# Attention on one core: two passes of 80 steps become one of 160, with the V product every second step, the softmax scaling on GpSimd and the first turned group evicted by VectorE

## The reference

```
def attend(q, k, v, scale):
    s = jnp.einsum('bhgqd,bhkd->bhgqk', q, k).astype(jnp.float32) * scale
    p = jax.nn.softmax(s, axis=-1).astype(v.dtype)
    return jnp.einsum('bhgqk,bhkd->bhgqd', p, v)
```

## Time and profile before

| | |
|---|---|
| time, 3 runs | 4382.3 us median (4377.97 to 4382.8) |
| profiled execution | span 4381.5 us from its first to its last instruction; no other time of this execution is given |
| busy in the span | PE 3800.6 us (87%), DVE 1762.5 (40%), ACT 1253.8 (29%), POOL 114.2 (3%) |
| granted TensorE clock, mean | 0.929 |
| attention, kind 0 | scores from 514.9 us, last product done by 813.8 |
| attention, kind 1 | scores from 831.1 us, last product done by 1165.3 |
| in kind 0 (298.9 us) | PE 260.69 busy, DVE 184.33, ACT 207.47, POOL 0 |
| in kind 1 (334.2 us) | PE 297.14 busy, DVE 187.29, ACT 213.36, POOL 0 |

### The profile page before, as it was taken

How to read it: one execution, slowest core, us unless ns; L and a number is a source line. 1 busy time by engine, 2 the same in 40 slices (tenths; PEclk the granted TensorE clock), 3 DMA queues, 4 the chain that set the end, 5 groups by cost and what they waited for, 6 DMA issues and landing times. The chain is left out here.

```text
span 4381.5 us, 45125 instructions
## 1 busy us (share of the span) xinstructions
PE 3800.6 (87%) x17768; PEld 2756.6 (63%) x17768; DVE 1762.5 (40%) x2388; ACT 1253.8 (29%) x2132; POOL 114.2 (3%) x80
## 2 busy tenths in 40 slices
PE   6687788788886999999996997749899878999997
PEld 2464366566674888888875685513344456888885
DVE  0321566555407333333345333953133234333334
ACT  2322467566524111111123132211100132221122
POOL 0000000000001000000000001300000010000001
PEclk7898899899997999999998998858999898999998
DMA  7532410110012111111122210021310121111112
GB/s 282 199 132 79 96 37 13 49 29 20 25 44 96 39 38 38 38 38 38 38 77 87 75 37 7 1 83 39 123 45 24 48 87 53 48 48 48 48 48 91
DMA packets 98138, 272.32 MB, mean 62 GB/s; under 512 B 18157, under 2 KB 33005, under 8 KB 93972
## 3 DMA queue, kind: packets, MB, share of 16 engines
q1 hardware_dynamic: 98004, 270.51, 18.5%
HBM read 220.41 MB, written 50.07 MB: 62 GB/s over the span
## 5 line engine op out<-in xcount | busy, mean ns | idle before, releaser
L514 PE MATMUL psum<-h_high,w_high 128*128 128x512 f32 (+1 forms) x1280 | 473.5, 370 | 51.5 <-DVE w_low L593 51.5
L514 PE MATMUL psum<-h_low,w_high 128*128 128x512 f32 (+1 forms) x1280 | 473.1, 370 | 0.0
L514 PE MATMUL psum<-h_high,w_low 128*128 128x512 f32 (+1 forms) x1280 | 472.5, 369 | 0.0
L527 PE MATMUL psum<-hid_low,w_high 128*128 128x512 f32 (+1 forms) x1280 | 471.6, 368 | 0.0
L527 PE MATMUL psum<-hid_high,w_high 128*128 128x512 f32 (+1 forms) x1280 | 471.3, 368 | 0.0
L527 PE MATMUL psum<-hid_high,w_low 128*128 128x512 f32 (+1 forms) x1280 | 470.8, 368 | 0.0
L458 PE MATMUL psum<-h_high,w_high 128*128 128x512 f32 (+1 forms) x944 | 368.1, 390 | 50.8 <-DMA swap_halves<-in_swap_a_dram 26.3
L590 DVE TENSOR_TENSOR out<-out,psum 128x512 f32<-128x512 f32 x320 | 202.9, 634 | 463.1 <-PE psum L527 463.1
L458 PE MATMUL psum<-h_high,w_low 128*128 128x512 f32 (+1 forms) x944 | 349.4, 370 | 0.0
L458 PE MATMUL psum<-h_low,w_high 128*128 128x512 f32 (+1 forms) x944 | 349.3, 370 | 0.0
L540 ACT ACTIVATE w_high<-w_raw 128x1024 fp32r<-128x1024 f32 x126 | 132.7, 1053 | 663.2 <-PE psum L527 662.8
(11 more groups left out here) (309 smaller groups left out, 5562.0 us busy)
## 6 DMA issues: line engine op xcount, KB each, us to landing
w_raw<-in_ff_w_dram SPq DMA_DIRECT2D x128, 512.0 KB
ada_ring<-in_ada_w_dram SPq DMA_DIRECT2D x24, 2048.0 KB, 10.8
scratch_x<-x SPq DMA_DIRECT2D x6, 2048.0 KB, 7.2
x<-scratch_x SPq DMA_DIRECT2D x6, 2048.0 KB
x<-in_x_dram SPq DMA_DIRECT2D x4, 2048.0 KB
w_raw<-in_w_out_dram SPq DMA_DIRECT2D x16, 512.0 KB
scratch_spectra<-spectrum_out SPq DMA_DIRECT2D x32, 256.0 KB, 2.0
filter_ring<-scratch_spectra SPq DMA_DIRECT2D x16, 512.0 KB, 3.7
```

The source lines that it names most:

```text
L514: mm = pe.matmul(g.ps[:, u % BANKS, 0:n], x[:, k, :], y[:, k, a:a + n], start=(k == 0 and i == 0), stop=(k == KT - 1 and i == 2))
L527: mm = pe.matmul(g.ps[:, BANKS + u % BANKS, 0:n], x[:, k * 2 + half, :], y[:, k, a:a + n], start=(k == 0 and i == 0), stop=(k == HT - 1 an ...
```

## The change

- One run over 8 pairs (4 of kind 0, then 4 of kind 1), `N` = 160 steps, in one set of buffers and semaphores. The first items of kind 1 are made ready during the last pair of kind 0: items are split at 25 steps instead of 21, besides the first pair's.
- A block is now 128 queries of both heads, 2 steps. `mix` is due in every even iteration and has 20 products of 128 columns instead of 256. The number of scores and transposes is the same.
- The turns lag 3 steps behind the scores (`LAG`) instead of 2. PE's order in an iteration becomes: scores of the first two banks, the first group of 4 transposes of x-3, the product if due, scores of the third bank, the other two groups.
- DVE copies the first turned group out of PSUM (L1195 in the new file), at the start of its iteration. ACT keeps the other two groups (L1253), and the product's result (L1248).
- GpSimd scales the probabilities (L1214) in place of DVE. DVE keeps maximum (L1200), reciprocal (L1206) and `split_item` (L1187).

```diff
-    ALL = [(pair, i) for pair in range(PAIRS) for i in range(S)]
+    ALL = [(pair, i) for pair in range(KINDS * PAIRS) for i in range(S)]
...
+    def block_due(x):
+        return (x - LAG - 2) // 2 if x % 2 == 0 and LAG + 2 <= x + 1 and 0 <= (x - LAG - 2) // 2 < N // 2 else None
+
+    use, act_turns = {}, {}
+    for x in range(N + LAG + 3):
+        if 0 <= x - LAG < N:
+            use["turn", x - LAG, 0] = len(use)
+        if block_due(x) is not None:
+            use["mix", block_due(x)] = len(use)
+        if 0 <= x - LAG < N:
+            for j in range(1, len(turns(x - LAG))):
+                use["turn", x - LAG, j] = len(use)
+                act_turns[x - LAG, j] = len(act_turns)
...
-                    for x in range(N + 3):
-                        if x < N:
-                            scores_of(x)
-                        if x > 2 and (x - 2) % PER_BLOCK == 0:
-                            mix((x - 3) // PER_BLOCK)
-                        if 2 <= x < N + 2:
-                            turn(x - 2)
...
+                def bank_free(r):
+                    if r < 2:
+                        return
+                    key = user[r - 2]
+                    if key[0] == "mix":
+                        pe.wait_ge(mixed_out, key[1] + 1)
+                    elif key[2] == 0:
+                        pe.wait_ge(first_out, key[1] + 1)
+                    else:
+                        pe.wait_ge(turned_out, act_turns[key[1], key[2]] + 1)
...
+                def mix(y):
+                    pair, b, _ = step(2 * y)
+                    lo, hi = keys_of(b)
+                    r = use["mix", y]
+                    bank_free(r)
+                    pe.wait_ge(first_out, 2 * y + 2)
+                    if act_turns_until(2 * y + 1):
+                        pe.wait_ge(turned_out, act_turns_until(2 * y + 1))
+                    pe.wait_ge(v_in[pair % 2], v_total(pair))
+                    for kt in range(lo, hi):
+                        for h in range(HEADS):
+                            mm = pe.matmul(g.ps[64 * h:64 * h + 64, 6 + r % 2, 0:P], v[:, pair % 2, kt, h, :], pt[:, y % 2, h, kt, :],
+                                           start=(kt == lo), stop=(kt == hi - 1))
+                    mm.then_inc(filled, 1)
+
+                for x in range(N + LAG + 3):
+                    if x < N:
+                        scores_of(x, 0, 2)
+                    if 0 <= x - LAG < N:
+                        turn(x - LAG, 0)
+                    if block_due(x) is not None:
+                        mix(block_due(x))
+                    if x < N:
+                        scores_of(x, 2, 3)
+                    if 0 <= x - LAG < N:
+                        for j in range(1, len(turns(x - LAG))):
+                            turn(x - LAG, j)
+
...
-                    for x in range(N + 1):
-                        if x < N:
-                            dve.wait_ge(scores, x + 1)
-                            if x >= 4:
-                                dve.wait_ge(exped, x - 3)
-                            flat = g.ps[:, 3 * (x % 2):3 * (x % 2) + 3, :].rearrange("p b n -> p (b n)")[:, 0:width(x)]
-                            dve.tensor_reduce(neg_max[:, x % 4:x % 4 + 1], flat, AX.X, ALU.max, negate=True).then_inc(maxed, 1)
-                        if x >= 1:
-                            y = x - 1
-                            dve.wait_ge(exped, y + 1)
-                            if y >= 4:
-                                dve.wait_ge(probs, y - 3)
-                            dve.reciprocal(inv[:, y % 4:y % 4 + 1], total[:, y % 4:y % 4 + 1]).then_inc(inverse, 1)
-                            dve.wait_ge(inverse, y + 1)
-                            dve.tensor_scalar(p[:, y % 3, 0:width(y)], p[:, y % 3, 0:width(y)], inv[:, y % 4:y % 4 + 1], None, ALU.mult).then_inc(probs, 1)
-                        if x < N and split_at(x):
-                            split_item(*split_at(x))
...
+                for x in range(N + LAG):
+                    if 0 <= x - LAG:
+                        dst, src = turned_to(x - LAG, 0)
+                        dve.wait_ge(filled, use["turn", x - LAG, 0] + 1)
+                        dve.tensor_copy(dst, src).then_inc(first_out, 1)
+                    if x < N:
+                        dve.wait_ge(scores, x + 1)
+                        if x >= 4:
+                            dve.wait_ge(exped, x - 3)
+                        dve.tensor_reduce(neg_max[:, x % 4:x % 4 + 1], scores_flat(x), AX.X, ALU.max, negate=True).then_inc(maxed, 1)
+                    if 1 <= x <= N:
+                        y = x - 1
+                        dve.wait_ge(exped, y + 1)
+                        if y >= 4:
+                            dve.wait_ge(probs, y - 3)
+                        dve.reciprocal(inv[:, y % 4:y % 4 + 1], total[:, y % 4:y % 4 + 1]).then_inc(inverse, 1)
+                    if x < N and split_at(x):
+                        split_item(*split_at(x))
+
+            @block.gpsimd
+            def _(pool):
+                for y in range(N):
+                    pool.wait_ge(inverse, y + 1)
+                    pool.tensor_scalar(p[:, y % 3, 0:width(y)], p[:, y % 3, 0:width(y)], inv[:, y % 4:y % 4 + 1], None, ALU.mult).then_inc(probs, 1)
...
+                for x in range(N + LAG + 3):
+                    if 1 <= x <= N:
+                        y = x - 1
+                        act.wait_ge(maxed, y + 1)
+                        if y >= 3:
+
+                            act.wait_ge(filled, last_turn(y - 3) + 1)
+                        if y >= 4:
+                            act.wait_ge(inverse, y - 3)
+                        act.activation(p[:, y % 3, 0:width(y)], scores_flat(y), ACT.Exp, bias=neg_max[:, y % 4:y % 4 + 1],
+                                       accum_out=total[:, y % 4:y % 4 + 1]).then_inc(exped, 1)
+                        if split_at(y):
+                            round_item(*split_at(y))
+                    if block_due(x) is not None:
+                        y = block_due(x)
+                        pair, b, _ = step(2 * y)
                         r = use["mix", y]
                         act.wait_ge(filled, r + 1)
-                        act.activation(out[:, kind * PAIRS + pair, b * QB:(b + 1) * QB], g.ps[:, 6 + r % 2, 0:QB], ACT.Copy).then_inc(emptied, 1)
-
-                    for n in range(I):
```

More of the change, by code:

```diff
@@ L1000, in keys_of, with kind_of, step @@
+    COPIES = (2, 1)
+    ROWS = (slice(0, P), slice(0, B_DK))
+    jobs = [(pair, n) for pair in range(KINDS * PAIRS) for n in range(len(ITEMS[pair // PAIRS]))]
+    job_of = {job: m for m, job in enumerate(jobs)}
+    def kind_of(pair):
+        return pair // PAIRS
+    def step(x):
+        pair, i = ALL[x]
+        return pair, i // HEADS, i % HEADS
     def keys_of(b):
-        return (0, KTILES) if b < LAT // QB else (LAT // P, KTILES)
-    def block_of(x):
-        return steps[ALL[x][1]][0]
+        return (0, KTILES) if b < LAT // P else (LAT // P, KTILES)
@@ new lines, in v_total @@
+    def v_total(pair):
+        return 16 * sum(COPIES[kind_of(i)] for i in range(pair % 2, pair + 1, 2))
+    def block_due(x):
[10 more added lines that the diff above has]
+                act_turns[x - LAG, j] = len(act_turns)
@@ L1089, in scores_of @@
                         if x >= 2:
                             pe.wait_ge(exped, x - 1)
-                        kh = 0 if kind == 0 else h
-                        passes = [(q_hi, k_hi), (q_hi, k_lo)] + ([(q_lo, k_hi)] if kind else [])
-                        for j, (a, n) in enumerate(parts):
-                            for m, (left, right) in enumerate(passes):
-                                mm = pe.matmul(g.ps[:, 3 * (x % 2) + j, 0:n], left[rows, s, h, qs], right[rows, s, kh, a:a + n],
-                                               start=(m == 0), stop=(m == len(passes) - 1))
-                            if j == len(parts) - 1:
-                                mm.then_inc(scores, 1)
@@ new lines, in scores_of @@
+                    passes = [(q_hi, k_hi), (q_hi, k_lo)] + ([(q_lo, k_hi)] if kind else [])
+                    for j, (a, n) in list(enumerate(parts))[first:last]:
+                        for m, (left, right) in enumerate(passes):
+                            mm = pe.matmul(g.ps[:, 3 * (x % 2) + j, 0:n], left[at, s, h, qs], right[at, s, kh, a:a + n],
+                                           start=(m == 0), stop=(m == len(passes) - 1))
+                        if j == len(parts) - 1:
+                            mm.then_inc(scores, 1)
@@ new lines, in turned_to, with scores_flat, _, split_item @@
+            def turned_to(x, j):
+                pair, b, h = step(x)
+                lo, hi = turns(x)[j]
+                y, r = x // 2, use["turn", x, j]
+                return pt[:, y % 2, h, lo:hi, :], g.ps[:, 6 + r % 2, 0:(hi - lo) * P].rearrange("p (k n) -> p k n", n=P)
+            def scores_flat(x):
```

(25 more changed lines are left out.)

232 lines of the change are left out of this document (91 added, 141 removed).

## The result

The changed kernel takes 4435.65 us (median of 4 runs, 4433.97 to 4437.33) against 4382.55 for the kernel before on the same chip: a ratio of 1.0127, 95% interval 1.0115 to 1.0139, so 53 us slower. The forecast was 4373, the range ended at 4412. The profiled execution has a span of 4433.7 us. The loss lies in attention: from the first score to the end of the last product it takes about 702 us (516.9 to 1219.1) instead of 650.4, where 641 was forecast.

A forecast was written before the change was run, and what follows sets the result against it. No engine was full for long; PE waited for evictions and, at splits, for DVE. Pairs -24.4, one run -22.3 and splits +37.5 gave -9.2 us against the 4381.5 span, so 4373 us, range 4336 to 4412.

The forecast's parts named there:

- the price of the scaling on GpSimd: Scaling of 1280 columns on GpSimd: taken as 2.41 us, between bounds of 0.887 and 4.08.
- the loop through GpSimd: Kind 0, two steps: maximum, reciprocal, scaling, first group, product, scores; 5.1 + 2.41 = 7.5 us, the longest loop.
- rival 2: GpSimd scaling sets attention's pace; each 0.1 us beyond 2.41 costs 3.2 us in kind 0; 4408 or 4456; chance 0.15.
- Steady state: Attention away from splits: two steps take 7.5 us in kind 0 and 8.4 in kind 1; pairs save 24.4 us.
- The splits: 25 item splits: DVE waits for ACT's rounding, delaying the copy; +57.8 us, +15 for clock, less 35.3 before: +37.5.
- Rival 1: Stalls at splits are milder, 1.7 us for each of 25 items: 4342 us, half way 4358; chance 0.25.
- Rival 3: Each of 25 split stalls drops the clock, +32 us, hand-overs +8: 4412 us; chance 0.16 with the dear product.
- The split that waits for GpSimd: `split_item` waits until the scaling ends: no cost at 2.41 us, 2.5 us for each 0.1 us more on GpSimd.
- One run of 160 steps: Merging both kinds removes the 17.3 us stretch between them and one fill and drain of 5: -22.3 us.
- The signs of being wrong: Attention: PE waits mostly for GpSimd, two-step period differs from 7.5 by over 0.3, or a split costs under 1.7 us.

The follow-up runs named there:

- e1: Changed kernel with DVE doing the reciprocal of step x-1 ahead of the maximum of step x: 4399.25 us, ratio 1.0037.
- e2: Changed kernel with the scaling back on DVE, behind the reciprocal: 4386.06 us, ratio 1.0007.
- e7: Changed kernel with GpSimd scaling only the first half of the columns, the rest left unscaled: 4378.48 us, ratio 0.9991.
- e3: Changed kernel with split_item on DVE moved from steps 5, 8, 11, 14 of a pair to 7, 9, 13, 15: 4367.23 us, ratio 0.9961.
- e6: Changed kernel with the scaling back on DVE and split_item one or two steps late: 4316.46 us, ratio 0.9846.
- e4: Kernel before with only both kinds merged into one run of 160 steps: 4367.56 us, ratio 0.9965.
- e5: Changed kernel with the reciprocal ahead of the maximum on DVE and split_item one or two steps late: 4339.06 us, ratio 0.9898.
- e9: Kernel before with only the scaling moved from DVE to GpSimd: 4522.95 us, ratio 1.0324.

## Why the prediction was wrong, step by step

**The step that failed is the price of the scaling on GpSimd.** I took 2.41 us from L1599, calling it nearest, when the rows offered 4.08 from L384 as well. Measured were 3.52 us for 1280 columns, 1.88 for 640 and 0.92 for 256, about 0.27 + 0.00254 a column. At 2.41 the loop through GpSimd came to 7.5 us, beside 7.4 for PE's own work; with 3.52 it is 8.7 and sets the pace in both kinds. Two operations of different kind do not bound a third by how alike they look; the price had to be carried as a range, with the weight in the middle (3.2) at least. At 3.2 us, by the prediction's own slopes (3.2 us in kind 0 and 2.5 at splits for each 0.1 us), the kernel comes out at 4373 + 7.9 x (3.2 + 2.5) = 4418, slower.

The Trainium skill, "GPSIMD Engine Reference", section 3, gave at most 2.8 us as I read it (an estimate), and its table of choices in section 4.1 calls one-input work roughly line-rate. Measured are 3.52 us, 4.0 times DVE's 0.887, so here the measurement decides against both.

**The mechanism of rival 2 was right.** Its loops, 5.1 and 5.2 us plus the scaling, give 8.62 and 8.72; measured 8.70 and 8.81. For 3.52 us its own prices, 3.2 us a tenth in kind 0 and 32 x (8.72 - 8.4) = 10 in kind 1, give 4373 + 36 + 10 = 4419. It left out the 2.5 us a tenth that the prediction had for the splits elsewhere; with these 28 us it is 4447. Measured is 4436, between the two. Its sum at 3.4 us was added up wrong as well: 32 + 6 = 38 us and 4411, not 34 and 4408. e1, e2 and e7 show the mechanism, each by another way out. Its chance of 0.15 was too low for a cost known only between 0.887 and 4.08.

**Steady state otherwise.** With the scaling short (e2, e7), periods are 7.06 and 8.43, against 7.4 and 8.4 forecast for PE. The period of kind 1 was right; in kind 0 my sum was 0.34 too long. Of that 2.58 - 2.39 = 0.19 is the wait for DVE's copy, which does not occur in the period of 7.02 of e1; the rest lies in the pieces. With the real scaling, a pair takes 693.56 - 614.99 = 78.6 us in kind 0 and 1011.86 - 931.80 = 80.1 in kind 1, read from e3, whose splits are free; 67.0 and 73.8 were forecast. That is 4 x 11.6 + 4 x 6.3 = 72 us too little; less the 6 us by which the splits were priced too dear, it makes 66 of a miss of 63.

Not all of the 72 is GpSimd's. In e6, with the scaling on DVE, a pair of kind 1, whose splits are free there, takes 890.95 - 815.24 = 75.7 us, and one of kind 0 takes 69.9, of which 3.3 go to splits, so 66.6. GpSimd's part is 4 x (78.6 - 66.6) + 4 x (80.1 - 75.7) = 66 us. The other 6 are 4 x 1.9 us more for pairs of kind 1 (75.7 for 73.8) less 4 x 0.4 for those of kind 0 (66.6 for 67.0). As the period of kind 1 was right, its 1.9 us lie in the steps around the narrow ones; which piece failed there is open. e7 gave back 57 of the 66, since splits cost 8 more in its shorter periods.

The lines of e3:

```profile
614.99 1.20 PE L1151 MATMUL psum<-probs_turned,v_pair 128*64 128x128 f32 x18
...
693.56 1.64 PE L1151 MATMUL psum<-probs_turned,v_pair 128*64 128x128 f32 x26
...
931.80 1.42 PE L1151 MATMUL psum<-probs_turned,v_pair 128*64 128x128 f32 x22
...
1011.86 1.31 PE L1151 MATMUL psum<-probs_turned,v_pair 128*64 128x128 f32 x20
```

**The splits** were to cost 57.8 + 15 = 72.8 us, and cost 67 here and 75 in e7. The size was right, and e3 gives it back. Its cause, the wait for the rounding with the copy behind it, holds for at most 47 of 68 us. The clock does fall behind a long wait, as I took it (0.50 behind the 4.18 us); how much of the 67 is clock was not tried apart. Rival 1 (milder stalls) is out: it had 1.7 us for a split, 2.7 were measured. Rival 3's dearer stalls are out as well.

**The split that waits for GpSimd** was in the prediction at no cost for 2.41, and 2.5 us for each tenth more. At 3.52 that is 28 us. It happened, but smaller: the 28 splits, the first pair's three among them, are 60.9 - 28 x 1.49 = 19 us longer in all, and 60.9 is the sum of L1187's four shapes.

**One run of 160 steps** was priced at -22.3. e4 gave -15.5 with the four more splits of the last pair of kind 0, which at the 1.7 us of the kernel before make -22.3 + 7 = -15.

**The signs of being wrong** that the prediction named: the period differs from 7.5 by over 0.3 (by 1.2), PE waits mostly for GpSimd (in the loop it does, but the list of waits has 31.2 us for it and 66.1 for the copy), a split costs under 1.7 us (it costs 2.7). The first one told it; the second would have missed it if read from the list.

## What to carry to other kernels

Before moving an operation to another engine, put its whole length into the loop that it stands in, for the range of lengths that the trace leaves open, and see at what length the loop passes the present pace; where that point lies inside the range, a short run of that one operation is worth more than the rest of the working. An engine can set the pace at 68% busy (479 of 707 us) while PE's waits for it are the smaller entry. An operation that waits for another engine should stand where that engine is already done: moving `split_item` by a step or two gave 68 us in the changed kernel (47 with one step alone) and 31 in the merged one, more than the 15.5 us of the merge, the one part of the change that was measured alone and gained.

## What the runs showed of the hardware

GpSimd's in-place multiplication by a column took 2.54 ns a column of float32 and 0.27 us besides, the mean of 3.52 us for 1280 columns the same within 0.01 us in the changed kernel, e1, e5 and e9. DVE's maxima and copies from PSUM beside it kept their 1.49 and 0.69 us.

DVE's subtraction with both inputs in SBUF and GpSimd's operation ran together for 0.7 us at most. Where the subtraction began in the last scaling of 3.52 us of its row, it ended 0.90 us behind that scaling (2.83 and 3.33 us for 1.49); where it began 0.55 us before the end of a scaling of 1.88 us, it took its usual 1.49. GpSimd stood for it as well: two scalings took 8.32 us for 7.03 where the subtraction came first, and 7.81 where it began in the first of them. The Trainium skill, "GPSIMD Engine Reference", key points, says that the interfaces are shared with VectorE instructions that have two SBUF inputs. The traces agree, and show that the one waits until the other's operation is all but over, not that both slow down.
